# A mixture-of-experts stage on one core: the first expert picks in two parts, woven into the products of expert 0

## The reference

```python
g_p, g_idx = lax.top_k(softmax(xt @ wg + bg), 1)       # one of 8 groups for each token
e_val, e_loc = lax.top_k(own group's 8 logits, 2)      # two of the group's 8 experts
weight = g_p * softmax(e_val)
# each expert, on the tokens that chose it:
y = (silu(xc @ w_gate[e]) * (xc @ w_up[e])) @ w_down[e]   # 2048 -> 256 -> 2048, 64 experts
# weighted, added back to each token; residual; last RMS norm
```

## Time and profile before

| | |
|---|---|
| median of 3 runs | 1949.46 us (1948.17 to 1949.99) |
| the profiled execution's own time | 1948.38 us |
| its span in the trace | 1946.6 us |
| TensorE busy | 1871.2 us, 96% of the span |
| TensorE weight loads | 1352.2 us, 69% |
| VectorE busy | 705.6 us, 36% |
| ScalarE busy | 584.6 us, 30% |
| GpSimd busy | 245.3 us, 13% |
| moved by DMA | 505.95 MB, mean 260 GB/s |

### The profile page before, as it was taken

The page is one execution under the profiler, slowest core; times in us unless marked ns, Lnnn a source line. Parts: engine busy times, 40 slices in busy tenths (PEclk is TensorE's granted clock), DMA queues, the critical chain, the costliest instruction groups (busy, mean ns, idle before and its releaser), DMA issues.

```text
span 1946.6 us, 28605 instructions
## 1 busy us (share of the span) xinstructions
PE 1871.2 (96%) x11936; PEld 1352.2 (69%) x11936; DVE 705.6 (36%) x1773; ACT 584.6 (30%) x1212; POOL 245.3 (13%) x208
## 2 busy tenths in 40 slices
PE   6999999999999999999999999989999899999997
PEld 6887777777777767788986666556665565656663
DVE  5331223333766668701042232322323222222222
ACT  5323333333443444422312232212212122121322
POOL 2433343433000000144100000000000000000000
PEclk9999999999999999999999999999999999999999
DMA  9554233234232232145489999999999999999995
GB/s 284 134 147 118 66 86 82 70 71 92 45 76 44 55 117 79 44 142 195 191 349 420 429 426 426 427 427 427 427 426 427 427 428 426 428 427 427 427 423 231
DMA packets 177745, 505.95 MB, mean 260 GB/s; under 512 B 52930, under 2 KB 136258, under 8 KB 151754
## 3 DMA queue, kind: packets, MB, share of 16 engines
q1 hardware_dynamic: 175306, 495.66, 66.5%
q0 software_dynamic: 2304, 8.39, 1.1%
HBM read 495.88 MB, written 16.53 MB: 263 GB/s over the span
## 4 chain that ended last, share of the span: by engine, by line
PE 81%; DMA 16%; ACT 1%; DVE 1%; issue 0%; SPq 0%; POOL 0%; POOLq 0%; ACTq 0%; DVEq 0%
PE banks L967 26%; PE banks L1375 13%; PE banks L1124 9%; PE banks L1400 8%; DMA x_region<-in_w_up 7%; DMA at_region<-in_w_up 7%; PE banks L1297 6%; PE banks L1376 3%; PE banks L1104 3%; PE banks L1076 2%; PE banks L1054 2%; PE banks L1346 2%; DMA ht_region<-in_w_up 2%; PE banks L1016 1%; PE banks L1215 1%; PE banks L1061 1%
## 5 line engine op out<-in xcount | busy, mean ns | idle before, releaser
L967 PE MATMUL banks<-ht_rounded,ring_rounded 128*128 128x512 f32 x1056 | 359.2, 394 | 0.7 <-ACT at_region L1538 0.7
L967 PEld LDWEIGHTS banks<-ht_rounded,ring_rounded 128*128 128x128 f32 x1056 | 195.1, 188 | 53.3 <-issue 13.8
L1375 PE MATMUL banks<-at_region,ht_region 128*64 128x256 f32 x800 | 179.0, 382 | 9.3 <-DMA at_region<-in_w_up 9.3
L864 POOL TENSOR_TENSOR ring_rounded<-ring_region,at_rounded 128x512 fp32r<-128x512 f32 (+1 forms) x92 | 115.9, 1291 | 511.3 <-ACT at_rounded L1477 511.3
L1376 PE MATMUL banks<-at_region,ht_region 128*64 128x256 f32 x768 | 175.3, 388 | 0.0
L2269 DVE SCALAR_TENSOR_TENSOR at_rounded<-banks,small,ring_rounded 128x512 fp32r<-128x512 f32 x128 | 96.1, 751 | 208.8 <-ACT ring_rounded L1763 207.9
L1763 ACT ACTIVATE ring_rounded<-banks,small 128x512 fp32r<-128x512 f32 x128 | 88.0, 687 | 241.3 <-PE banks L1400 241.3
L2262 DVE COPY consts<-banks 128x128 f32<-128x128 f32 x64 | 18.7, 292 | 388.1 <-PE banks L1385 388.1
L1375 PEld LDWEIGHTS banks<-at_region,ht_region 128*64 128x64 f32 x800 | 109.1, 138 | 67.3 <-issue 21.1
L967 PE MATMUL banks<-ht_rounded,at_rounded 128*128 128x512 f32 x352 | 142.7, 405 | 1.0 <-ACT at_region L1530 0.7
L1753 ACT ACTIVATE ring_region<-banks,consts 64x256 f32<-64x256 f32 x64 | 30.0, 469 | 364.4 <-PE banks L1376 364.1
(11 more groups left out here) (300 smaller groups left out, 3488.2 us busy)
## 6 DMA issues: line engine op xcount, KB each, us to landing
at_region<-in_w_gate SPq DMA_DIRECT2D x23, 2048.0 KB, 30.0
at_region<-in_w_up SPq DMA_DIRECT2D x22, 2048.0 KB, 27.6
at_region<-in_w_down SPq DMA_DIRECT2D x22, 2048.0 KB, 23.9
ring_region<-in_w_in SPq DMA_DIRECT2D x36, 1024.0 KB, 5.9
x_region<-in_w_down SPq DMA_DIRECT2D x17, 2048.0 KB, 26.6
x_region<-in_w_up SPq DMA_DIRECT2D x15, 2048.0 KB, 28.9
x_region<-in_w_gate SPq DMA_DIRECT2D x14, 2048.0 KB, 29.9
ring_region<-in_w_gate SPq DMA_DIRECT2D x9, 2048.0 KB, 32.6
```

Source lines behind the costliest of these rows:

```text
L864: ins = nc.gpsimd.tensor_tensor(w_low[n % RING][:, ks, 0:width], ring[n % RING][:, ks, 0:width], w_high[n % 2][:, ks, 0:width].bitcast(F32 ...
L967: ins = mm(out, w[:, k, 0:width], h[:, k, :], start=k == 0 and i == 0, stop=k == KT - 1 and i == 2)
L1375: mm(place[0:CAP, 0:D_EXPERT], x, gate[j], start=j == 0, stop=j == KT - 1)
```

## The change

1. The first half's picks (4 experts, 256 slots) of group 0 are made in two parts of 128 slots each (2 experts), with 16 picks each. VectorE builds `pick` in three instructions instead of one: 128, 128 and 256 slots.
2. Part 0: four picks are issued first (four banks); the other twelve stand inside the loop of gate and up of expert 0, one at each step j from 0 to 11, for j + 4.
3. The 8 tiny products of the norm's factor move behind gate and up of expert 0.
4. Part 1: 16 picks over three banks, between expert 0's gate and up and `place_marks`. VectorE and ScalarE copy them; on VectorE they stand behind the chain of the marks.
5. The filler before the ranks goes from 16 to 11 products.
6. The load of the third expert's up weights waits for `g_copied` (the gather has been issued) instead of the gather's landing.

```diff
+FIRST_PARTS = ((0, 2 * CAP), (2 * CAP, HALF))
+first_places = ((banks[:, 6, :], banks[:, 2, :], banks[:, 3, :], banks[:, 0, :]), (banks[:, 2, :], banks[:, 3, :], banks[:, 0, :]))
...
-            sp.wait_ge(xg_in[0], 16)
+            sp.wait_ge(g_copied, 1)
...
-            keep_busy(16)
+            keep_busy(11)
...
+            def pick_first(part, j):
+                lo, hi = FIRST_PARTS[part]
+                if j == 0:
+                    pe.wait_ge(first_picks, part + 1)
+                if part == 0 and j == 0:
+                    pe.wait_ge(idx_ready, 1)
+                    pe.wait_ge(xg_in[0], 16)
+                places = first_places[part]
+                at = j - len(places)
+                if at >= 0:
+                    pe.wait_ge(xT_v if at % 2 else xT_a, part * KT // 2 + at // 2 + 1)
+                mm(places[j % len(places)][:, 0:hi - lo], first_rows[:, j, :], pick[:, lo:hi], start=True, stop=True).then_inc(picked, 1)
...
                 for j in range(KT):
                     if picks is not None:
                         pe.wait_ge(xT_v if j % 2 else xT_a, done + j // 2 + 1)
+                    if begins_all(c, g) and e8 == 0 and j + len(first_places[0]) < KT:
+                        pick_first(0, j + len(first_places[0]))
                     x = xT[:, 0 if fast(c) else e8 // 4, j, e8 % 4 * CAP:(e8 % 4 + 1) * CAP]
                     mm(place[0:CAP, 0:D_EXPERT], x, gate[j], start=j == 0, stop=j == KT - 1)
                     ins = mm(place[CAP:2 * CAP, 0:D_EXPERT], x, up[j], start=j == 0, stop=j == KT - 1)
...
+                if e8 == 0 and begins_all(c, g):
+                    pe.wait_ge(pick_ready, 1)
+                    ins = root_of_slots()
                 ins.then_inc(gu_done, 1)
...
                     if begins_all(c, g) and e8 == 0:
+                        for part in range(1, len(FIRST_PARTS)):
+                            for j in range(KT):
+                                pick_first(part, j)
                         place_marks(c)
...
-            pick_half(0, 0)
+            for j in range(len(first_places[0])):
+                pick_first(0, j)
...
-            build_pick(0, 0)
+            v.tensor_copy(group_slots, slot_of_row[:, 0:PER]).then_inc(own_slots, 1)
+            dve.wait_ge(own_slots, 1)
+            pick_by_slots = pick.rearrange("p (e s) -> p e s", e=PER)
+            for lo, hi in FIRST_PARTS:
+                es = slice(lo // CAP, hi // CAP)
+                v.tensor_tensor(pick_by_slots[:, es, :], bcast(iota, 1, es.stop - es.start),
+                                bcast(group_slots[:, es], 2, CAP), ALU.is_equal).then_inc(first_picks, 1)
+            es = slice(HALF // CAP, PER)
+            v.tensor_tensor(pick_by_slots[:, es, :], bcast(iota, 1, PER - es.start), bcast(group_slots[:, es], 2, CAP),
+                            ALU.is_equal).then_inc(pick_ready, 1)
```

More of the change, by code:

```diff
@@ L1356, in gate_up @@
                 picks = e8 // (PER // 2) if fast(c) and e8 % (PER // 2) == 0 else None
-                done = copies_ahead(c, g) + (picks or 0) * (KT // 2)
+                done = copies_ahead(c, g)
+                if picks:
+                    done += half_after(g, picks)
+                if begins_all(c, g) and any(e8 * CAP == lo for lo, _ in FIRST_PARTS[1:]):
+                    picks, done = -1, KT // 2
                 if e8 == 0 and not fast(c):
@@ L1360, in gate_up @@
                     pe.wait_ge(xT_v, done + 8)
-                if picks is not None:
+                if picks is not None and (g or e8 >= PER // 2):
                     i = max(j for j in range(KT) if TURN4[j] == 1)
@@ L1364, in gate_up, with root_of_slots @@
                 fence(c, g)
-                if e8 == 0:
+                def root_of_slots():
                     for i in range(PER):
-                        mm(place[0:CAP, RSTD + i * N_GROUPS:RSTD + (i + 1) * N_GROUPS], pick[:, i * CAP:(i + 1) * CAP], row_rstd,
-                           start=True, stop=True)
+                        ins = mm(place[0:CAP, RSTD + i * N_GROUPS:RSTD + (i + 1) * N_GROUPS], pick[:, i * CAP:(i + 1) * CAP],
+                                 row_rstd, start=True, stop=True)
+                    return ins
+                if e8 == 0 and not begins_all(c, g):
+                    root_of_slots()
                 for j in range(KT):
@@ L1729, in copy_half, with copy_first @@
             def copy_half(g, h):
-                place, turn = half_places(g, h)
                 for j in range(0, KT, 2):
-                    act.wait_ge(picked, picks_ahead(0, g) + h * KT + j + 1)
-                    fn(xT[:, 0, j, :], place[turn[j]][:, 0:HALF], ACT.Copy, scale=ln2_sb[:, j:j + 1]).then_inc(xT_a, 1)
+                    act.wait_ge(picked, picks_ahead(0, g) + 2 * half_after(g, h) + j + 1)
+                    fn(xT[:, 0, j, :], whole_banks[TURN4[j]][:, 0:HALF], ACT.Copy, scale=ln2_sb[:, j:j + 1]).then_inc(xT_a, 1)
+            def copy_first(part):
+                lo, hi = FIRST_PARTS[part]
+                for j in range(0, KT, 2):
+                    act.wait_ge(picked, part * KT + j + 1)
+                    fn(xT[:, 0, j, lo:hi], first_places[part][j % len(first_places[part])][:, 0:hi - lo], ACT.Copy, scale=ln2_sb[:, j:j + 1]).then_inc(xT_a, 1)
             def square_rows(c, g, b):
@@ L1790, in _ @@
             fn(r_tmp[:, 4], r_tmp[:, 3], ACT.Exp).then_inc(e_exped, 1)
-            copy_half(0, 0)
+            for part in range(len(FIRST_PARTS)):
+                copy_first(part)
             for g in range(N_GROUPS):
@@ L2198, in copy_half, with copy_first @@
             def copy_half(g, h):
-                place, turn = half_places(g, h)
                 for j in range(1, KT, 2):
-                    dve.wait_ge(picked, picks_ahead(0, g) + h * KT + j + 1)
-                    v.tensor_scalar(xT[:, 0, j, :], place[turn[j]][:, 0:HALF], ln2_sb[:, j:j + 1], None, ALU.mult)\
+                    dve.wait_ge(picked, picks_ahead(0, g) + 2 * half_after(g, h) + j + 1)
+                    v.tensor_scalar(xT[:, 0, j, :], whole_banks[TURN4[j]][:, 0:HALF], ln2_sb[:, j:j + 1], None, ALU.mult)\
                         .then_inc(xT_v, 1)
-            copy_half(0, 0)
+            def copy_first(part):
+                lo, hi = FIRST_PARTS[part]
+                for j in range(1, KT, 2):
+                    dve.wait_ge(picked, part * KT + j + 1)
+                    v.tensor_scalar(xT[:, 0, j, lo:hi], first_places[part][j % len(first_places[part])][:, 0:hi - lo], ln2_sb[:, j:j + 1], None, ALU.mult)\
+                        .then_inc(xT_v, 1)
+            copy_first(0)
             link(v.tensor_tensor(cand2, tops, bcast(ranks, 1, 2), ALU.mult))
```

29 lines of the change are left out of this document (16 added, 13 removed).

## The result

The changed kernel takes **1962.16 us** (median of 6, 1960.41 to 1965.68) against 1949.72 us of the kernel before in the same comparison (median of 6, 1947.28 to 1952.44): a ratio of 1.0067, 95% interval 1.0055 to 1.0078, or 12.4 us more. Forecast were 1958.9 us, 9.4 us more, in a range of 1946.5 to 1965. The profiled execution took 1963.45 us (span 1961.7), 15.1 us more than the profiled one before.

The account below looks back on a forecast made before the run. A TensorE chain from first pick to the load release at 1053.67 us was taken as the bound. Terms +0.7, +1.5, +7.1 and 0.1 for a form change gave +9.4, so 1958.9 us on the median; range 1946.5 to 1965.

Parts of the forecast that it names:

- The bound: TensorE's chain from first pick (986.47 us) to the load release at 1053.67 us; shifting it shifts the end as much.
- The start: Up to the first pick: filler 1.1 us less, gather landing 7.8 us after issue, so first pick 0.7 us later.
- Part 0: Picks woven into expert 0's gate and up: 16.8 us with tiny products, against 15.3 before, so +1.5 us.
- Part 1: 16 more picks between tiny products and marks, held by three banks and VectorE's marks chain: +7.1 us.
- the trip between the forms: In expert 0's loop, switching between 128*64 and 128*128 products and back costs 0.44 us at each of twelve steps.
- its upper end: Top of the range, 1965 us; two clock falls, 3.4 us, were kept for it and left out of the sum.
- the gap between the two issues: The single hole between SyncE's issues around 1054 us moves to about 1063 and grows to several microseconds.
- steps 1.10 us apart: Starts of gate's steps 0 to 11 of expert 0 lie 1.1 us apart.
- marks at 1011 us: `place_marks`, ahead of expert 1's gate and up, starts near 1011 us instead of 1001.74.
- A: The weight stream counts from its start, so earlier loads give 4 to 5 us less, about 1944.8 us; chance 0.08.
- B: Weaving in expert 0's loop is cheap and later picks take 3.6 us: sum -1.4, 1948.1 us; chance 0.20.
- C: The gather suffers in full, landing at 990.8 us, +3.6 on the forecast: 1962.5 to 1965.9 us; chance 0.12.

Follow-up runs that it names:

- filler_after_marks: The kernel before with 22 more filler products on TensorE between the marks and expert 1's gate and up; 1954.35 us, ratio 1.0027.
- two_parts_unwoven: The changed kernel with all 16 picks of the first part made in a row ahead of expert 0's gate and up; 1956.89 us, ratio 1.0047.
- dose_other_form: The kernel before with one 128*128 product ahead of each of the first twelve steps of expert 1's gate and up; 1956.92 us, ratio 1.0035.
- dose_same_form: The kernel before with one 128*64 product ahead of each of the first twelve steps of expert 1's gate and up; 1952.72 us, ratio 1.0016.
- chain_behind_copies: The changed kernel with VectorE's marks chain behind its copies of the second part and the marks behind expert 1's gate and up; 1961.13 us, ratio 1.0076.
- filler_before_picks: The changed kernel with 12 filler products instead of 6 ahead of the picks; 1961.60 us, ratio 1.0071.
- late_load: The changed kernel with the third expert's up load waiting for the gather's landing again; 1960.18 us, ratio 1.0057.

## Why the prediction came out as it did

**The bound was right.** The end moved by what the release moved (15.07 us the span, 15.13 us the release), and filler_after_marks, where only TensorE got more work, shows that one makes the other.

**The start**, forecast +0.7, by one term taken off and one added, and neither is as forecast. The 1.1 us for five filler products are there only when the clock falls under the filler, as it did in the trace that the forecast was read from; at the full clock VectorE's `chosen` comes last ahead of the ranks, and they are worth nothing. The gather with the load beside it was taken to land 7.8 us after its issue and lands after 6.8 to 7.2. Counted from the gather's issue the first pick is 0.2 us earlier than in the profile before (7.11, 6.91), and 1.1 us later than the same code without the fall (5.79).

**Part 0**, forecast 16.8 us: 18.8 without a fall of the clock. This is the step that failed, at "one of 128 slots should take 0.22": it took the time of a pick for a matter of its columns. A pick of 128 slots takes 0.44 us, as one of 256 does. Two mistakes ran against each other: the pick was 0.22 too cheap, the trip between the forms, 0.44 for 0.35, was 0.09 too dear, and the step came out as 1.10 for 1.215. That makes 1.4 us in twelve steps. About 0.7 us more lie ahead of the loop, where four picks take 4 x 0.44 = 1.8 us and 1.05 was put.

**Part 1**, forecast 7.1 us: 8.2 to 8.3. The number is near by luck, for the mechanism was wrong. Neither the return of three banks nor VectorE's chain makes its 7.2 us; 16 picks at 0.44 us do, and a fourth bank changes nothing. The chain adds 1.0 us on top, as a wait of 0.77 us after the fourth pick.

With the measured prices the sum is: 16 picks more, 7.0; eleven round trips more than the unwoven order has, 3.85; VectorE's chain, 1.0: **+11.9 us**. With the start, -0.2 to +1.1, it is 11.7 to 13.0, beside the 12.4 measured. The forecast, +9.4, had 1.5 and 7.1 us for parts 0 and 1, which are 3.5 and 8.2 to 8.3. Each term has its own kernel: two_parts_unwoven (+6.97 in its chain), dose_other_form less dose_same_form (4.2 for twelve), chain_behind_copies (+10.76, that is 3.8 more than two_parts_unwoven and 0.9 to 1.2 less than filler_before_picks and late_load). The profiled changed kernel lies above that, +14.26, by its 6.8 us of low clock in part 0 (2.2 us, 21.0 against 18.8), such a fall as the forecast kept for its upper end.

**The signs.** Right: the first pick at 987.33 us; the hole of 985 to 990 us filled (share 1.02 for 0.84) without use; copies of part 1 only behind the chain. Half right: the gap between the two issues moved, but to 1068.80 us, not 1063, and the hole in it did not grow to several microseconds (a share of 0.72 from 1068.13 to 1071.13 us, of 0.83 from 1053 to 1056 us before, so 0.8 us missing for 0.5): the engines ran dry earlier instead, at 1015 to 1020 us, because expert 1's quarters were released later. Wrong: steps 1.10 us apart, marks at 1011 us (1016.67), the gather's landing after 7 to 9 us (6.8).

**The rivals.** A fell with filler_after_marks and with the holes of 990 to 1025 us, which grew and cost nothing beside the chain. B, cheap weaving, fell twice: the trip has its price, and even free trips (two_parts_unwoven) leave +7. C had the right time, 1962.5, by the wrong cause: the gather lost 1.4 to 2.2 us, not 6.

## What to carry to other kernels

Before a product is cut into narrower ones, read its weight loads beside it: where they fill its time, half the columns cost the same and each part pays in full. Weaving products of another form into a loop pays for every change: here a round trip costs as much as one and a half products of the filler, while a same-form product in the same place costs its own time and no more. Read the clock of the stretch, too, before taking a saving off it: the filler's 1.1 us existed only where the clock had fallen. A number that comes out near is no proof of its mechanism: one more bank would have been the cheap question to ask.

## What the runs showed of the hardware

- Weight loads of the gathered rows (128x128, float32) follow each other at 0.22 us, those of the identity at 0.11 us, and those of line 1177's transposes, from the same place and at the same stride, at 0.12 us.
- The picks keep their pace at half the granted clock: 7.22 us with 3.4 us of 0.50 in it, 7.18 us without. The filler does not: 32 records take 5.45 us for 3.82.
- A round trip between products of form 128*64 and 128*128 costs 0.35 us; a dose in the same form costs 0.22 us a product and nothing beside it.
- A gather of 128 rows of 8 KB takes 5.0 to 5.4 us to its landing alone and 6.8 to 7.2 us beside a load in rows of 8 KB; under whole loads in rows of 16 KB it took 10.5 to 13.0 us.
- At the low clock the woven step takes 1.79 us for 1.215: the stretch from gate to the next pick takes 1.06 us for 0.58, the pick 0.73 for 0.63. Waits of TensorE for the gather, 0.98 to 1.47 us long, were followed by a low stretch in three of six traces.
